# A two-stream feed-forward block: 768 columns cut at the boundary of the streams instead of in the middle

## The reference

```python
def swiglu(h, w_in, w_out):
    gate, up = jnp.split(h @ w_in, 2, axis=-1)
    return (jax.nn.silu(gate) * up) @ w_out

m = (silu(c) @ w_ada + b_ada).reshape(b, 1, 9, d)       # mc: the same of c_ctx
x = x + 0.5 * m[2] * swiglu(modulate(rmsnorm(x, norm_ffn1), m[0], m[1]), w_ffn1_in, w_ffn1_out)
ctx = ctx + 0.5 * mc[2] * swiglu(modulate(rmsnorm(ctx, norm_ffn1), mc[0], mc[1]), w_ffn1_in, w_ffn1_out)
```

## Time and profile before

| | |
|---|---|
| Median of three runs | 3197.62 us |
| Span of the profiled execution | 3207.6 us (10.0 above the median) |
| PE busy | 2779.5 us (87%) |
| DVE busy | 1687.7 us (53%) |
| POOL busy | 1147.5 us (36%) |
| ACT busy | 889.7 us (28%) |
| Mean granted clock of PE | 0.953 |

### The profile page before, as it was taken

The page is one execution under the profiler, slowest core; times in us unless marked ns, Lnnn a source line. Parts: engine busy times, 40 slices in busy tenths (PEclk is TensorE's granted clock), DMA queues, the critical chain, the costliest instruction groups (busy, mean ns, idle before and its releaser), DMA issues.

```text
span 3207.6 us, 30181 instructions
## 1 busy us (share of the span) xinstructions
PE 2779.5 (87%) x11160; PEld 1902.4 (59%) x11160; DVE 1687.7 (53%) x3622; ACT 889.7 (28%) x1683; POOL 1147.5 (36%) x763
## 2 busy tenths in 40 slices
PE   5999999979988999989987889998787777777876
PEld 3999989967667887768846555544233223232332
DVE  3766652022726702121146267776777777767765
ACT  3111122123532223232132333323222222222221
POOL 1222222223924444232210135544444444444441
PEclk8999999989999999989987899999999999999999
DMA  5455531212014522212100249999999999999996
GB/s 201 145 176 179 177 120 55 61 58 73 27 66 146 174 100 86 92 40 66 55 34 1 66 186 388 403 416 426 427 427 427 426 427 427 427 427 427 427 427 293
DMA packets 126958, 722.12 MB, mean 225 GB/s; under 512 B 15205, under 2 KB 17517, under 8 KB 60141
## 3 DMA queue, kind: packets, MB, share of 16 engines
q0 software_dynamic: 73728, 536.90, 40.0%
q1 hardware_dynamic: 37448, 127.67, 11.6%
q10 hardware_dynamic: 15652, 55.90, 5.5%
HBM read 718.31 MB, written 2.10 MB: 225 GB/s over the span
## 4 chain that ended last, share of the span: by engine, by line
PE 58%; DMA 27%; DVE 9%; ACT 3%; issue 2%; POOL 1%; SPq 0%; DVEq 0%; ACTq 0%; POOLq 0%
PE acc L571 14%; PE acc L572 14%; PE acc L573 14%; DMA hid<-in_peer_rows,squares 8%; DMA wring<-in_peer_rows,squares 7%; DMA resid<-in_peer_rows,squares 5%; DMA arena<-in_peer_rows,squares 4%; PE sums L1025 4%; PE acc L1025 3%; PE sums L512 2%; DVE hid L1684 2%; DVE hid_parts L1690 1%; DMA modw<-in_peer_rows,squares 1%; ACT hid L1087 1%; DVE hid L2282 1%
## 5 line engine op out<-in xcount | busy, mean ns | idle before, releaser
L2447 POOL TENSOR_TENSOR wring_parts<-wring,wring_parts 128x1024 fp32r<-128x1024 f32 (+1 forms) x215 | 517.0, 2416 | 1317.1 <-ACT wring_parts L1087 1316.9
L571 PE MATMUL acc<-hid_parts,wring_parts 128*128 128x384 f32 (+2 forms) x2088 | 780.6, 374 | 80.8 <-DVE hid_parts L1690 60.6
L573 PE MATMUL acc<-hid_parts,wring_parts 128*128 128x384 f32 (+2 forms) x2088 | 756.7, 362 | 0.0
L572 PE MATMUL acc<-hid_parts,wring_parts 128*128 128x384 f32 (+1 forms) x1656 | 601.3, 363 | 0.0
L571 PEld LDWEIGHTS acc<-hid_parts,wring_parts 128*128 128x128 f32 (+1 forms) x2088 | 397.6, 190 | 157.7 <-issue 70.7
L573 PEld LDWEIGHTS acc<-hid_parts,wring_parts 128*128 128x128 f32 (+1 forms) x2088 | 398.4, 191 | 36.8
L1087 ACT ACTIVATE wring_parts<-wring 128x1024 fp32r<-128x1024 f32 (+1 forms) x215 | 222.1, 1040 | 605.2 <-DMA wring<-in_w_ffn_out 219.4
L572 PEld LDWEIGHTS acc<-hid_parts,wring_parts 128*128 128x128 f32 x1656 | 316.3, 191 | 31.3 <-issue 5.5
L2459 POOL DMA_INDIRECT arena<-in_peer_rows,squares x180 | 198.9, 1105 | 242.1 <-PE acc L1025 149.8
L1087 ACT ACTIVATE hid<-hid 128x2 f32<-128x2 f32 (+2 forms) x293 | 67.0, 229 | 765.4 <-DVE arena L2282 237.6
L2459 POOL DMA_INDIRECT wring<-in_peer_rows,squares x158 | 178.4, 1129 | 199.3 <-PE acc L1025 144.6
(11 more groups left out here) (402 smaller groups left out, 4412.3 us busy)
## 6 DMA issues: line engine op xcount, KB each, us to landing
wring<-in_w_ffn_in SPq DMA_DIRECT2D x88, 512.0 KB, 5.5
modw<-in_w_ada ACTq DMA_DIRECT2D x56, 512.0 KB, 3.9
modw<-in_w_mod ACTq DMA_DIRECT2D x48, 512.0 KB, 4.0
wring<-in_w_ffn_out SPq DMA_DIRECT2D x32, 512.0 KB, 3.5
wring<-in_w_in SPq DMA_DIRECT2D x28, 512.0 KB, 3.5
wring<-in_w_mix_in SPq DMA_DIRECT2D x18, 512.0 KB, 3.4
wring<-in_peer_w_q SPq DMA_DIRECT2D x16, 512.0 KB, 5.8
hid<-in_w_ada SPq DMA_DIRECT2D x6, 1024.0 KB, 17.4
```

What stands on the lines that cost most here:

```text
L571: nc.tensor.matmul(o, wh, high, start=first, stop=False)
L572: nc.tensor.matmul(o, wh, low, start=False, stop=False)
L573: return nc.tensor.matmul(o, wl, high, start=False, stop=last)
L2447: nc.gpsimd.tensor_tensor(Wlor[:, p, 0:blocks, 0:cols], Wlo[:, p, 0:blocks, 0:cols], Whir[:, p, 0:blocks, 0:cols], ALU.subtract).then_inc( ...
```

## The change

The two halves of 384 columns become two spans: the sequence's 512 and the context's 256. `ffn_in`, `ffn_out`, `silus` and `swiglu` get a tuple of spans instead of a width and a number of halves, the high parts of the hidden tiles are cut at column 512, and the residual has two instructions per tile instead of three. The second feed-forward gets one span of 512, which is what it had. The number of matmuls, weight loads, DMAs and units stays.

```diff
--- before.py
+++ after.py
...
+BOTH_STREAMS, SEQUENCE = ((0, T), (T, TC)), ((0, T),)
...
-        hi_ff768 = ([(tmp_parts[:, 0:HALF], tmp_parts[:, HALF:TC]), (rstd_parts[:, 0:HALF], rstd_parts[:, HALF:TC])]
-                    + [(hid_parts[:, TC * f:TC * f + HALF], hid_parts[:, TC * f + HALF:TC * (f + 1)]) for f in range(16)]
-                    + [(modw_parts[:, TC * f:TC * f + HALF], modw_parts[:, TC * f + HALF:TC * (f + 1)]) for f in range(2)]
-                    + [(modw_parts[:, 2 * TC:2 * TC + HALF], modrows_parts[:, 0:HALF]), (squares_parts[:, 0:HALF], squares_parts[:, HALF:TC])])
+        hi_ff768 = ([(tmp_parts[:, 0:T], tmp_parts[:, T:TC]), (rstd_parts[:, 0:T], rstd_parts[:, T:TC])]
+                    + [(hid_parts[:, TC * f:TC * f + T], hid_parts[:, TC * f + T:TC * (f + 1)]) for f in range(16)]
+                    + [(modw_parts[:, TC * f:TC * f + T], modw_parts[:, TC * f + T:TC * (f + 1)]) for f in range(2)]
+                    + [(modw_parts[:, 2 * TC:2 * TC + T], modrows_parts[:, 0:C]), (squares_parts[:, 0:T], squares_parts[:, T:TC])])
...
-            def ffn_in(name, width, halves, h_before):
+            def ffn_in(name, spans, h_before):
+                halves = len(spans)
...
-                                at = slice(hf * width, (hf + 1) * width)
-                                mm = split_product(acc[:, b + m, 0:width], s % W_RING, k, P, high[:, k, at], low[:, k, at], k == 0, k == KD - 1)
+                                lo, end = spans[hf]
+                                mm = split_product(acc[:, b + m, 0:end - lo], s % W_RING, k, P, high[:, k, lo:end], low[:, k, lo:end], k == 0, k == KD - 1)
...
-            def ffn_out(name, width, high, low, ff_before, between):
+            def ffn_out(name, spans, high, low, ff_before, between):
...
-                            for hf in range(len(high[f])):
-                                mm = split_product(acc[:, b + hf, 0:width], s % W_RING, f - first, P, high[f][hf],
-                                                   low[:, f, hf * width:(hf + 1) * width], f == 0, f == FT - 1)
+                            for hf, (lo, end) in enumerate(spans):
+                                mm = split_product(acc[:, b + hf, 0:end - lo], s % W_RING, f - first, P, high[f][hf],
+                                                   low[:, f, lo:end], f == 0, f == FT - 1)
-            ffn_in("ffn1_in", HALF, 2, 0)
+            ffn_in("ffn1_in", BOTH_STREAMS, 0)
-            ffn_out("ffn1_out", HALF, hi_ff768, lo_ff768, 0, between_stat)
+            ffn_out("ffn1_out", BOTH_STREAMS, hi_ff768, lo_ff768, 0, between_stat)
...
-            ffn_in("ffn2_in", T, 1, 16)
+            ffn_in("ffn2_in", SEQUENCE, 16)
-            ffn_out("ffn2_out", T, hi_ff512, lo_ff512, FT, between_stat2)
+            ffn_out("ffn2_out", SEQUENCE, hi_ff512, lo_ff512, FT, between_stat2)
...
             def high_of_ff(ff, high, f):
-                width = ff.shape[2] // len(high[f])
-                for hf, dst in enumerate(high[f]):
-                    ins = run(dst, ff[:, f, hf * width:(hf + 1) * width], ACT.Copy)
+                for dst, (lo, end) in zip(high[f], BOTH_STREAMS):
+                    ins = run(dst, ff[:, f, lo:end], ACT.Copy)
-            def silus(name, width, halves, first_quarter, stop_quarter, out_name, ff, high):
+            def silus(name, spans, first_quarter, stop_quarter, out_name, ff, high):
+                halves = len(spans)
                 for u in range(units * FT // 2):
+                    width = spans[u % halves][1] - spans[u % halves][0]
...
-            silus("ffn1_in", HALF, 2, 0, EARLY_PAIRS * QUARTERS, "ffn1_out", ff768, hi_ff768)
+            silus("ffn1_in", BOTH_STREAMS, 0, EARLY_PAIRS * QUARTERS, "ffn1_out", ff768, hi_ff768)
...
-            silus("ffn2_in", T, 1, EARLY_PAIRS * QUARTERS, N_PAIRS_OF_GROUPS * QUARTERS, "ffn2_out", ff512, hi_ff512)
+            silus("ffn2_in", SEQUENCE, EARLY_PAIRS * QUARTERS, N_PAIRS_OF_GROUPS * QUARTERS, "ffn2_out", ff512, hi_ff512)
...
-                width = ff.shape[2] // len(high[f])
-                for hf, part in enumerate(high[f]):
-                    at = slice(hf * width, (hf + 1) * width)
-                    ins = V.tensor_tensor(low[:, f, at], ff[:, f, at], part, ALU.subtract)
+                for part, (lo, end) in zip(high[f], BOTH_STREAMS):
+                    ins = V.tensor_tensor(low[:, f, lo:end], ff[:, f, lo:end], part, ALU.subtract)
-            def swiglu(name, width, sides, done, first_pair, stop_pair, out_name, ff, high, low, before):
-                base = UNIT[name]
+            def swiglu(name, spans, done, first_pair, stop_pair, out_name, ff, high, low, before):
+                base, sides = UNIT[name], len(spans)
                 for u in range(2 * sides * FT // 2):
-                    f, hf = u // sides, u % sides
+                    f, (lo, end) = u // sides, spans[u % sides]
+                    width = end - lo
-                    free(V.tensor_tensor(arena[:, (f * sides + hf) * width:(f * sides + hf + 1) * width], sg[:, (base + u) % 2, 0:width],
+                    free(V.tensor_tensor(ff[:, f, lo:end], sg[:, (base + u) % 2, 0:width],
...
-                    parts = [(0, 0, T, 0, 0)] if sides == 1 else [(0, 0, HALF, 0, 0), (0, HALF, T, 1, 0), (1, T, TC, 1, T - HALF)]
+                    parts = [(0, 0, T, 0, 0), (1, T, TC, 1, 0)][:sides]
...
-            swiglu("ffn1_in", HALF, 2, 0, 0, EARLY_PAIRS, "ffn1_out", ff768, hi_ff768, lo_ff768, 0)
+            swiglu("ffn1_in", BOTH_STREAMS, 0, 0, EARLY_PAIRS, "ffn1_out", ff768, hi_ff768, lo_ff768, 0)
...
-            swiglu("ffn2_in", T, 1, 44, EARLY_PAIRS, N_PAIRS_OF_GROUPS, "ffn2_out", ff512, hi_ff512, lo_ff512, FT)
+            swiglu("ffn2_in", SEQUENCE, 44, EARLY_PAIRS, N_PAIRS_OF_GROUPS, "ffn2_out", ff512, hi_ff512, lo_ff512, FT)
```

## The result

The changed kernel takes 3245.45 us (median of four runs, 3238.37 to 3254.84), beside 3197.61 us for the kernel before on the same chip (four runs, 3191.43 to 3202.46): a ratio of 1.0141, 95% interval 1.0119 to 1.0162, so 38 to 52 us slower. Forecast were 3215 us and a range of 3190 to 3232. The direction was right; the forecast rise of 17 us is less than half of the measured one. The profiled execution spans 3252.9 us, 45.3 more than that of before.

What follows compares the result with a forecast made beforehand. PE's matmul stream was taken to bound the steady loop. Waits +18.9, first step -5.6, clock +3.9, residual -0.1 and streams 0 gave +17.1 us on 3197.6, say 3215; range 3190 to 3232.

Steps and rivals of the forecast that it cites:

- The streams: First feed-forward's matmuls on PE: 256 columns take 0.120 us, a 512 and 256 pair 0.347 as before, zero change.
- rival 2: Narrow matmul slower than 0.120 us: at 0.130, 3225 to 3235 us; at 0.173, about 3290; chance 0.12 (slower than 0.125).
- The mechanism: Modulation load issued at b+0.4 (b: narrow unit's end), behind the tile's; DVE's last quarter meets POOL, PE waits at mod_add.
- Rivals 1 and 3: 1: rhythm harmless, only first-step gain left, 3192 us, chance 0.20. 3: waits in half the steps, 3204 to 3208, 0.12.
- The wait per step: PE waits at mod_add in ffn1_in's steps 2 to 10, 2.1 us each, +18.9 us in all.
- the landing: After the narrow unit's end b, modulation data land at about b+6, POOL starts at b+6.5, quarters are done at b+12.9.
- The clock: PE's clock behind the new holes: three falls in ten, 1.3 us each, +3.9 us; bounds 0 and +15.
- The first step: Start of ffn1_in: earlier units, a narrow unit behind, hole shrinking from 4.4 to 2.1 us, less half clock: -5.6 us.
- Sum for ffn1_in: Forecast total for the first product of the first feed-forward: waits +18.9, first step -5.6, clock +3.9 us.
- The residual and ffn1_out: Residual in 16 instructions instead of 24, only the last tile's on the path: -0.1 us; ffn1_out's streams unchanged.
- The rest: Profiled execution's 10.0 us above the median taken as no part of the first feed-forward block; difference carried over to the median.

Runs made afterwards that it cites:

- pool_yields: Changed kernel, but in ffn1_in POOL starts a tile's subtraction only after the DVE finishes the quarters of the unit that freed it; 3205.72 us, 1.0013 of the kernel before.

## Why the prediction was wrong

**Right.** The streams: 0.120 us for 256 columns, rival 2 has nothing. (The two distances of the earlier trace rows give 0.422 ns per column and not 0.418, so the line itself gives 0.119; that is 2 us in the sum.) The mechanism: ten waits at mod_add for the DVE. In seven steps the modulation load is issued at b+0.4 (306.99 against 306.6) and POOL's subtractions lie over the last two instructions, 2.89 and 2.82 us; in the other three it is a load still later. Rivals 1 and 3 fall: all steps wait. pool_yields shows the whole loss in ffn1_in to be this collision. The Trainium skill, "SBUF — State Buffer", section "Who interferes with whom", has the rule that the second to issue fully blocks. The trace agrees: the quarters' instructions that start behind one of POOL's end 0.54 to 0.56 us behind it (317.57 against 317.01, 320.31 against 319.77).

**The wait per step** (18.9 us) was mis-sized. Steps 2 to 10 have holes of 2.3 to 3.6 us, 25.6 in all instead of 18.9. The step that failed is the landing, in the prediction's words "POOL starts at about b+6.5" and "data land at about b+6": in the earlier trace rows the tile's data took 5.4 us from issue. At 306.76 they take 6.4, and those of the modulation 6.4 from 306.99. POOL starts at b+7.7 there (b+7.0 to b+7.8 in the nine steps), and a blocked last instruction ends half a microsecond behind POOL's second subtraction: the quarters are done at b+13.7, there and in the mean of the nine, instead of b+12.9. I had taken the landing times of the one collision that I had, and did not ask what they hang on.

**The clock** (3.9 us) was mis-sized too: it fell to half behind five of these nine holes (0.60 from 320.5 to 324.5), not three in ten, at 1.6 us each. At the same place of each step the shift against the kernel before grows from -2.0 us behind the first mod_add to +31.7 behind the tenth; of the 33.7, 25.6 are holes, and the other 8.1 are the lower clock.

**The first step** (-5.6 us) failed as a term. In the first execution it was worth -2.0, since the hole stayed at 4.2 us. I had given step 1 the wait of the others, but the DVE is one quarter further behind there: both modulation loads that mod_add waits for are issued behind the tiles' (107.17), at 107.79 and 110.55, and when the first has landed the DVE has two quarters to go, eight instructions from 113.52 to 122.07, the first two of them beside POOL.

```profile
107.79 3.09 ACTq L1173 DMA_DIRECT2D modw<-in_w_ada  x2
...
112.34 5.20 POOL L2449 TENSOR_TENSOR wring_parts<-wring,wring_parts 128x1024 fp32r<-128x1024 f32 x2 [8.98 <-ACT wring_parts L1089]
...
113.52 1.77 DVE L1746 SCALAR_TENSOR_TENSOR squares<-modw,cond,squares 128x512 f32<-128x512 f32 x1 [1.75 <-DMA modw<-in_w_ada]
115.21 2.88 DVE L1746 SCALAR_TENSOR_TENSOR arena<-modw,cond,arena 128x512 f32<-128x512 f32 x1
...
122.12 1.01 PE L557 MATMUL misc<-tmp,cst 128*2 128x512 f32 x1 [4.22 <-DVE arena L1746]
```

And against the second execution of the kernel before, which like two more kernels with the same ffn1_in has no such hole, it costs +4.4 (-1.8 against -6.2 in the table). The prediction credited the change with a hole that was one execution's, not the kernel's.

**Sum for ffn1_in:** -2.0 + 25.6 + 8.1, less 1.8 by which the shift swings within a step (a wide unit ends later than a half of 384, the narrow one behind it makes up for it): +29.9 against the first execution, as in the table. Against the second execution of before it is +36.7, and +40.8 for the second of the changed kernel. Forecast was +17.2.

**The residual and ffn1_out** (-0.1 us): +1.4 instead, from PE's own pace, of which the prediction had a straight line and no row.

**The rest.** I took the surplus of 10.0 us in the profiled execution of before as no part of this block. Seven of it were: its first step. Against the second execution of before, the two of the changed kernel stand 38.3 and 41.3 us behind at the end of ffn1_out, where the two first executions differ by 31.1; the medians differ by 48 us (45 and 39 by the two ratios). So some 7 us of the miss come from taking one profile's hole for the kernel's, as many as from the longer waits (25.6 instead of 18.9). Behind ffn1_out the executions drift by up to 14 us either way (the second of before got 11 us further ahead there, the first of the changed kernel fell 14 further behind), also in kernels that change nothing there, so I ascribe none of it to the change; for one execution each it can't be told.

## What to carry to other kernels

Where two engines' work is interleaved by issue times, a change that costs nothing in sums can cross an edge: look for the two transfers or instructions whose order it turns, and price the turned order from a row in which it is turned, with what each then takes. A hole that a profile shows once is a property of that execution until a second one shows it; before crediting a change with its removal, price the change without it. And when one queue's load gates the critical path, let the bulk loads of other queues wait for its issue: 1 us of delay on the tiles here gave back about 40 (3204.83 us against 3245.73, each from its own chip; by the ratios 37).

## What the hardware showed that I had not expected

- What a load takes hangs on its neighbours. By the page of the changed kernel (KB each, median us from issue to landing) the modulation loads take 3.9 us and the tiles', of which two always go together, 5.7. In ffn1_in of all runs, a modulation load that goes 0.3 to 0.6 us ahead of a tile's has landed after 4.0 to 4.5 us, and one that goes 0.6 to 1.2 ahead after 3.9 to 5.4; less than 0.15 us ahead it took 4.7 to 6.4, and up to 2 us behind 5.1 to 7.0.

```profile
wring<-in_w_ffn_in SPq DMA_DIRECT2D x88, 512.0 KB, 5.7
modw<-in_w_ada ACTq DMA_DIRECT2D x56, 512.0 KB, 3.9
```

- One start 0.04 us behind POOL's cost the DVE 2.1 us (2.86 for 0.75), and it can differ between executions of one kernel: in the first step of the kernel before POOL met two instructions once and one the other time.
- Outside such places the pace repeats to the hundredth: 940 matmuls of ffn1_out take 168.07 us in five executions and 166.63 in three, give or take 0.01.
